# Seven block products instead of eight in both feed-forward layers, the weight sums made on GpSimd

## The reference, cut to what matters

```python
D_MODEL = 1024; SEQ = 512; N_META = 16; D_FF = 2816

def swiglu_ffn(h, w_gate, w_up, w_down):
    return (jax.nn.silu(h @ w_gate) * (h @ w_up)) @ w_down

for i in range(DEPTH):                       # DEPTH = 2
    h = rms_norm(h_res, ln_mix[i])
    mix = s5_mixer(h, ...) if i % 2 == 0 else sink_window_attention(h, ...)
    h_res = h_res + mix
    h_res = h_res + swiglu_ffn(rms_norm(h_res, ln_ffn[i]), w_gate[i], w_up[i], w_down[i])
out = rms_norm(h_res, ln_f)[:, N_META:]
```

## Time and profile before

| | |
|---|---|
| median of three runs | 1177.77 us (1177.47 to 1181.88) |
| span of the profiled execution | 1177.9 us |
| PE busy | 1140.4 us, 97% |
| PE weight loads | 1025.8 us, 87% |
| DVE busy | 553.8 us, 47% |
| ACT busy | 412.4 us, 35% |
| POOL busy | 174.8 us, 15% |
| layer 0's feed-forward, first product to last | about 239 to 628 us |
| layer 1's feed-forward | about 807 to 1168 us |
| share of PE's product line in the chain that ended last | 79% |

### The profile page before, as it was taken

One profiled execution on the slowest core, in us unless ns is written; L12 is line 12 of the kernel. 1 busy time (PEld: TensorE's weight loads), 2 busy tenths in 40 slices (PEclk: granted clock), 3 DMA queues, 4 the chain that ended last, 5 costly groups with the idle time before them and its releaser, 6 DMA issues.

```text
span 1177.9 us, 20443 instructions
## 1 busy us (share of the span) xinstructions
PE 1140.4 (97%) x8362; PEld 1025.8 (87%) x8362; DVE 553.8 (47%) x845; ACT 412.4 (35%) x701; POOL 174.8 (15%) x114
## 2 busy tenths in 40 slices
PE   5799999999999999999999899989999999999998
PEld 5688899999999999999999676678888888888887
DVE  7978444443344333444334355455443434434444
ACT  6823232332222222233323455443322223223332
POOL 4699000011111111100000000001111111110000
PEclk9999899999999999999999999999999999999999
DMA  7164333222323232222323211022333233223332
GB/s 141 24 163 111 87 109 108 72 89 91 98 80 100 78 107 71 76 83 91 98 81 126 72 37 42 32 72 72 108 107 99 79 107 107 75 73 97 98 98 94
DMA packets 119387, 104.63 MB, mean 89 GB/s; under 512 B 21868, under 2 KB 117216, under 8 KB 119008
## 3 DMA queue, kind: packets, MB, share of 16 engines
q1 hardware_dynamic: 110120, 99.85, 27.9%
q10 hardware_dynamic: 9216, 4.06, 1.5%
HBM read 98.11 MB, written 5.24 MB: 88 GB/s over the span
## 4 chain that ended last, share of the span: by engine, by line
PE 90%; DVE 4%; DMA 2%; ACT 1%; POOL 1%; issue 1%; SPq 0%; ACTq 0%; DVEq 0%; POOLq 0%
PE banks L1380 79%; PE banks L1520 1%; PE banks L1457 1%; PE banks L1510 1%; PE banks L1731 1%; PE banks L1734 1%; PE banks L1752 1%; PE banks L1721 1%; PE banks L1458 1%; DMA y_dram<-y_act 1%; PE banks L1746 1%; PE banks L1472 0%; POOL col_mag L499 0%; PE banks L1720 0%; ACTq L719 0%
## 5 line engine op out<-in xcount | busy, mean ns | idle before, releaser
L587 ACT CAST w_high<-raw 128x1024 fp32r<-128x1024 f32 x186 | 195.0, 1049 | 572.1 <-PE banks L1380 572.1
L945 DVE TENSOR_TENSOR w_low<-raw,w_high 128x1024 fp32r<-128x1024 f32 x186 | 228.2, 1228 | 208.3 <-ACT w_high L587 208.3
L1380 PE MATMUL banks<-x_high,w_high 128*128 128x512 f32 (+2 forms) x1184 | 321.0, 324 | 1.0 <-DVE x_low L1173 1.0
L1380 PE MATMUL banks<-x_high,w_low 128*128 128x512 f32 (+2 forms) x1184 | 318.5, 322 | 0.0
L1380 PE MATMUL banks<-x_low,w_high 128*128 128x512 f32 (+2 forms) x1184 | 317.7, 321 | 0.0
L1380 PEld LDWEIGHTS banks<-x_high,w_high 128*128 128x128 f32 x1184 | 198.9, 189 | 19.4 <-issue 2.2
L1380 PEld LDWEIGHTS banks<-x_low,w_high 128*128 128x128 f32 x1184 | 198.9, 188 | 16.1
L1380 PEld LDWEIGHTS banks<-x_high,w_low 128*128 128x128 f32 x1184 | 198.2, 188 | 16.8
L1380 PE MATMUL banks<-a_high,w_high 128*128 128x256 f32 (+2 forms) x533 | 141.2, 318 | 0.0
L1380 PE MATMUL banks<-a_low,w_high 128*128 128x256 f32 (+2 forms) x533 | 141.1, 318 | 0.0
L1380 PE MATMUL banks<-a_high,w_low 128*128 128x256 f32 (+2 forms) x533 | 141.1, 318 | 0.0
(11 more groups left out here) (288 smaller groups left out, 1249.3 us busy)
## 6 DMA issues: line engine op xcount, KB each, us to landing
raw<-in_ffn_w_gate SPq DMA_DIRECT2D x22, 1024.0 KB, 5.3
raw<-in_ffn_w_up SPq DMA_DIRECT2D x22, 1024.0 KB, 5.3
raw<-in_ffn_w_down SPq DMA_DIRECT2D x16, 768.0 KB, 4.4
raw<-in_ffn_w_down SPq DMA_DIRECT2D x16, 640.0 KB, 4.1
raw<-in_attn_w_qkv SPq DMA_DIRECT2D x6, 1024.0 KB, 5.0
k_toep<-k_dram SPq DMA_DIRECT2D x64, 64.0 KB, 2.6
raw<-in_ssm_w_glu_b SPq DMA_DIRECT2D x4, 1024.0 KB, 5.5
raw<-in_ssm_w_glu_a SPq DMA_DIRECT2D x4, 1024.0 KB, 5.8
```

The source lines that it names most:

```text
L587: nc.scalar.copy(high[:, j], raw[:, slot, :, j * P:(j + 1) * P]).then_inc(w_rounded, 1)
L945: nc.vector.tensor_tensor(low[:, j], raw[:, slot, :, j * P:(j + 1) * P], high[:, j], ALU.subtract).then_inc(w_split, 1)
L1380: ins = nc.tensor.matmul(banks[:, bank + h, b0:b0 + cn], w[:, j, k, :], xx[:, first_k + k, c0 + base:c0 + base + cn], start=start and k == ...
```

## The change

Each feed-forward layer becomes 34 units. A unit is one tile of 2 kp x 256 weights: kp = 4 pairs of input blocks (3 in four of the down units) by a pair of output blocks. The tokens are cut into two halves (264 each in layer 0, 256 in layer 1). So the product of a unit is a 2 x 2 by 2 x 2 block product, and it is made with seven block products in place of eight (the scheme of Strassen, in Winograd's form). With `w` the four blocks (0 and 1 from the first row of blocks, 2 and 3 from the second):

- weights: four block sums: `s13` = (w0 + w1, w3 + w1), `s2` = w0 + w3 + w1, `s4` = w2 + s2, all on GpSimd, next to the plain blocks w0, w2 (the column) and w3 (the corner). All seven are rounded by ScalarE and split by VectorE;
- activations: three plain blocks and four sums or differences (T1 to T4) for each pair of rows, seven slots in `xs_high`, `xs_low` and, between up and down, `a_high`, `a_low`;
- results: ScalarE copies three products out of their banks, VectorE combines them to the four corners of the output.

A layer is staged: four pairs of up units, a down stage over pairs 0 to 2, four pairs of up units, a down stage over pairs 3 to 6, three pairs of up units, a down stage over pairs 7 to 10. A down stage has four units, each adding to two rows of `residual`. A ring of SLOTS = 5 pairs of activations takes the place of 22 kept blocks.

TensorE's order in a unit is column w0, first sum, s2, column w2, second sum, corner, s4. The weight parts have one slot each, so a part of the next unit is rounded when TensorE has done this unit's product with it. GpSimd no longer scales the gate; VectorE does. ScalarE's, VectorE's, GpSimd's and SyncE's loops are unrolled.

The last quad of the mixer's output and the last blocks of the attention's output now also carry the preparation of unit 0 (`round_s2`, `split_s2` and the others), and the input rows are prepared in pairs (`pair_first`, `pair_second`) with seven slots.

The core of the diff:

```diff
+        def blocks_of(g, kp):
+            return raw[:, g % 2, 0:2 * kp, :].rearrange("p (k i) (o c) -> p k (i o) c", i=2, o=2)
...
+            def sums13(g, kp):
+                pool.wait_ge(unit_loaded[g % 2], 16 * (g // 2 + 1))
+                if g >= 1:
+                    pool.wait_ge(t_split, 5 * (g - 1) + (5 if g % UNITS == 1 else 2))
+                w = blocks_of(g, kp)
+                nc.gpsimd.tensor_tensor(s13[:, 0:kp], w[:, :, 0::3, :], w[:, :, 1, :].unsqueeze(2).to_broadcast([P, kp, 2, P]),
+                                        ALU.add).then_inc(s13_made, 1)
+            def sum2(g, kp):
+                pool.wait_ge(s13_made, g + 1)
+                if g >= 1:
+                    pool.wait_ge(t_split, 5 * (g - 1) + 3)
+                    pool.wait_ge(s4_made, g)
+                nc.gpsimd.tensor_tensor(s24[:, 0, 0:kp], blocks_of(g, kp)[:, :, 0, :], s13[:, 0:kp, 1, :], ALU.add).then_inc(s2_made, 1)
+            def sum4(g, kp):
+                pool.wait_ge(s2_made, g + 1)
+                if g >= 1:
+                    pool.wait_ge(t_split, 5 * g)
+                nc.gpsimd.tensor_tensor(s24[:, 1, 0:kp], blocks_of(g, kp)[:, :, 2, :], s24[:, 0, 0:kp], ALU.add).then_inc(s4_made, 1)
...
+            def round_s2(g, kp):
+                if g % UNITS > 0:
+                    act.wait_ge(part_done, 7 * (g - 1) + 3)
+                act.wait_ge(s2_made, g + 1)
+                nc.scalar.copy(w2_high[:, 0, 0:kp, :], s24[:, 0, 0:kp, :]).then_inc(t_rounded, 1)
...
+                def copy_parts(g):
+                    act.wait_ge(part_done, 7 * g + 1)
+                    act.wait_ge(c11_made, g)
+                    nc.scalar.copy(copied_part(0, n), bank_part(Y_BANK[g % 2], n)).then_inc(part_copied, 1)
+                    act.wait_ge(part_done, 7 * g + 2)
+                    act.wait_ge(c22_made, g)
+                    nc.scalar.copy(copied_part(1, n), bank_part(W_BANK[g % 2], n)).then_inc(part_copied, 1)
+                def copy_sum(g):
+                    act.wait_ge(part_done, 7 * g + 3)
+                    act.wait_ge(c21_made, g)
+                    nc.scalar.copy(copied_part(2, n), bank_part(Y_BANK[g % 2], n)).then_inc(part_copied, 1)
+                def prepare(unit):
+                    g, kp = UNITS * layer + unit, pairs_of(unit)
+                    round_s2(g, kp)
+                    round_column(g, kp)
+                    round_sums(g, kp)
+                    round_corner(g, kp)
+                    round_s4(g, kp)
+                def unit_behind_acts(unit, i):
+                    copy_parts(UNITS * layer + unit)
+                    round_acts(i)
+                    copy_sum(UNITS * layer + unit)
+                    round_act_sums(i)
+                    prepare(unit + 1)
+                def up_behind_gate(unit, i):
+                    copy_parts(UNITS * layer + unit)
+                    silu(i)
+                    copy_sum(UNITS * layer + unit)
+                    prepare(unit + 1)
...
+                def gate_unit(i):
+                    g, kp = UNITS * layer + up_unit(i), pairs_of(up_unit(i) + 1)
+                    first_corner(g, gate_part(n, 0, 0))
+                    last_corner(g, gate_part(n, 1, 1))
...
+                    split_column(g + 1, kp)
+                    low_corner(g, gate_part(n, 1, 0))
+                    split_sums(g + 1, kp)
+                    split_s2(g + 1, kp)
...
+                    dve.wait_ge(part_done, 7 * g + 7)
+                    TT(gate_part(n, 0, 1), bank_part(Y_BANK[g % 2], n), rstd_part(n, 1), ALU.mult).then_inc(set_free, 1)
+                    split_corner(g + 1, kp)
+                    split_s4(g + 1, kp)
...
+                    TT(gate_part(n, 0, 0), gate_part(n, 0, 0), rstd_part(n, 0), ALU.mult)
+                    TT(gate[:, 1, 0:n], gate[:, 1, 0:n], rstd_row[:, t0:L], ALU.mult).then_inc(gate_pre, 1)
+                def up_products(i):
...
+                    corner, low, far = (bank_part(b[g % 2], n) for b in (X_BANK, W_BANK, V_BANK))
+                    TT(corner, corner, gate_part(n, 0, 0), ALU.mult)
+                    TT(low, low, gate_part(n, 1, 0), ALU.mult)
+                    mark(TT(far, far, gate_part(n, 1, 1), ALU.mult))
...
+                    TT(act_t[:, 0, 0:h], corner, cross, ALU.subtract).then_inc(act_ready, 1)
+                    TT(act_t[:, 2, 0:h], cross, far, ALU.subtract)
...
+                    STT(act_t[:, 1, 0:h], act_t[:, 0, 0:h], -1.0, far, ALU.mult, ALU.subtract).then_inc(act_ready, 1)
...
+                    TT(act_t[:, 3, 0:h], low, act_t[:, 1, 0:h], ALU.add).then_inc(act_ready, 1)
...
+            def unit_products(g, parity, x, slots, n, first=0, need_b11=None, need_all=None, mean_at=None, spread_at=None):
+                y, w, v = Y_BANK[parity], W_BANK[parity], X_BANK[parity]
+                if first == 0:
+                    pe.wait_ge(set_free, g - 1)
+                pe.wait_ge(t_split, 5 * g + (4 if first == 1 else 1))
+                part(col, 0, x, slots, B11, y, n, start=True, need=need_b11)
...
+                pe.wait_ge(t_split, 5 * g + (5 if first == 1 else 2))
+                part(sums, 0, x, slots, T3, w, n, start=True, need=need_all)
+                pe.wait_ge(t_split, 5 * g + (5 if first == 1 else 3))
+                pe.wait_ge(part_copied, 3 * g + 1)
+                part(w2, 0, x, slots, T2, y, n)
+                part(col, 1, x, slots, B21, v, n, start=True)
...
+                pe.wait_ge(part_copied, 3 * g + 3)
+                part(sums, 1, x, slots, T1, y, n)
+                pe.wait_ge(t_split, 5 * g + (5 if first == 1 else 4))
+                part(w2, 1, x, slots, T4, w, n)
+                pe.wait_ge(t_split, 5 * g + 5)
+                pe.wait_ge(c22_made, g + 1)
+                part(w2, 2, x, slots, B22, y, n)
```

More of the change, by code:

```diff
@@ L798, in _ @@
             for i in range(N_GLU):
                 gated(QUAD_GLU + i, i, ACT.Sigmoid, L)
-                for j in range(2):
-                    updated(2 * i + j, 2 * i + j, L, "ln_ffn0")
+                if i == N_GLU - 1:
+                    round_s2(0, KP)
+                    round_corner(0, KP)
+                    round_s4(0, KP)
+                    act.wait_ge(w_used, 4 * N_GLU - 1)
+                    round_column(0, KP)
+                pair_first(0, i, L, "ln_ffn0")
+                if i == N_GLU - 1:
+                    act.wait_ge(w_used, 4 * N_GLU)
+                    round_sums(0, KP)
@@ L837, in feed_forward @@
                 if layer == 0:
-                    with act.Fori(0, N_DOWN, 1) as i:
-                        down(i, False)
-                else:
-                    with act.Fori(0, N_DOWN - 1, 1) as i:
-                        down(i, False)
-                    for off in range(6):
-                        round_weights(QUAD_DOWN[layer] + 2 * (N_DOWN - 1), 2 + off)
-                    updated(adds0 + KB - 2, KB - 2, n, gain)
-                    for h in range(2):
-                        r_h = half_tokens(h)
-                        act.wait_ge(added, adds0 + KB - 1 + h + 1)
-                        nc.scalar.activation(gate[:, 0, r_h], residual[:, KB - 1, r_h], ACT.Square).then_inc(squared, 1)
@@ L851, in _ @@
-            feed_forward(0, L, N_GLU, KB, 0, "ln_mix1")
+                    for m in range(KB - 2, KB):
+                        normed(m)
+                        squared_of(KB + m, m, n)
+                else:
+                    for q in range(2):
+                        act.wait_ge(last_ready, q + 1)
+                        nc.scalar.activation(last_sq[:, :, q * h:(q + 1) * h], residual[:, KB - 2:, half_tokens(q)],
+                                             ACT.Square).then_inc(squared, 1)
@@ L1618, in last_mean @@
                     nc.tensor.matmul(banks[:, MEAN_BANKS[h], t:t + 1], sq_sum[:, tokens], ones[:, 0:1], start=True, stop=False)
-                    ins = nc.tensor.matmul(banks[:, MEAN_BANKS[h], t:t + 1], gate[:, 0, tokens], ones[:, 0:1], start=False, stop=True)
+                    for j in range(2):
+                        ins = nc.tensor.matmul(banks[:, MEAN_BANKS[h], t:t + 1], last_sq[:, j, t * P:(t + 1) * P], ones[:, 0:1],
+                                               start=False, stop=j == 1)
                 ins.then_inc(mean_summed, 1)
@@ L1688, in _, with part @@
-            feed_forward(0, L, N_GLU, KB, 0, [(gate_ready, 2 * N_GLU - 1), (gate_ready, 2 * N_GLU)])
-            first_quad(QUAD_KV, 1, L, [(added, 2 * KB - 1), (added, 2 * KB)], None)
+            col = (col_high(w_high, KP), col_high(w_low, KP))
+            sums = (sum_high(w_high, KP), sum_high(w_low, KP))
+            w2 = tuple(w[:].rearrange("p s k c -> p k s c") for w in (w2_high, w2_low))
+            def part(w, i, x, slots, c, bank, n, start=False, need=None):
+                for m, slot in enumerate(slots):
+                    if need is not None:
+                        need(m)
+                    for a, b in ((0, 0), (0, 1), (1, 0)):
```

(4 more changed lines are left out.)

716 lines of the change are left out of this document (508 added, 208 removed).

## The result

The changed kernel takes 1377.1 us (median of 4 runs, 1371.9 to 1379.0) against 1179.4 us (4 runs, 1177.5 to 1181.9) for the kernel before on the same chip. The ratio is 1.168, 95% interval 1.165 to 1.171. It is slower, as forecast, but by 198 us where 135 had been forecast, and the time lies 11 us above the range. The profiled execution has a span of 1377.2 us, so it can be read without a shift.

The account below looks back on a forecast made before the run. TensorE was taken to bound the kernel before, and a VectorE-ScalarE-TensorE loop with waits for GpSimd's port the changed one. 1177.9 + 110 (layers) + 10 (outside) + 15 (clock) = 1313 us, range 1215 to 1366.

Parts of the forecast that it names:

- The bound before and TensorE's floor: Feed-forward layers: TensorE bounds the kernel before; its floor after the change is 20.5 us a pair of gate and up units.
- fourth rival: TensorE: narrow products dearer than 0.1219 us through new rows' place in SBUF; result as forecast; chance 0.05.
- first rival: VectorE and GpSimd: the exclusion does not act on this pattern, TensorE is the bound, about 1135 us; chance 0.08.
- The exclusion: VectorE instructions with two SBUF operands wait out whole GpSimd instructions that read SBUF; 7.0 us a pair in the loop.
- second rival: VectorE keeps the port between its own instructions, GpSimd takes what is left; 1222 us; chance 0.15.
- The loop of a pair: VectorE, ScalarE and TensorE's fifth product, per gate and up pair: 20.0 us alone, 27.0 with waits for GpSimd.
- The clock: TensorE drops to half clock after some gaps in up and gate units: 15 us taken, between 0 and 66.
- third rival: TensorE: the clock falls in nearly every gap, 66 us, giving 1364 us; chance 0.12.
- Outside the layers: First unit's preparation +3 us and +4 in layer 1, keys +1, the end +2: 10 us.
- The edges of the stages: Down units: 10.8 us each, 8.9 with three pairs of rows, waits behind GpSimd included.
- What would show it right: Changed profile: TensorE at 75 to 80%, idle before the fifth product; 512-element splits 1.7 to 2.6 us; matmul spacing 0.12.
- The stall before the last down stage: Last down stage of each layer: waits for the newest activations, about 11 us once a layer.

Follow-up runs that it names:

- e1: Changed kernel with every GpSimd weight sum cut to 4 of 128 columns; 1146.4 us, 0.971 of the kernel before.
- e4: Changed kernel with each GpSimd weight sum replaced by three memsets of its tile; 1153.5 us, 0.978 of the kernel before.
- e8: Changed kernel with each GpSimd weight sum replaced by two copies with one SBUF input each; 1234.9 us, 1.049 of the kernel before.
- e2: Changed kernel with 20 filling matmuls ahead of the fifth product of gate and up units but the first two; 1337.7 us, 1.134 of the kernel before.
- e10: Changed kernel with silu over one of the two gate rows, the other left out; 1358.1 us, 1.151 of the kernel before.
- e12: Changed kernel with 12 filling matmuls ahead of the fifth product of gate and up units but the first two; 1335.7 us, 1.132 of the kernel before.

## Why the prediction was right or wrong

- *The bound before and TensorE's floor:* right. With the exclusion gone (e1) the pair takes 20.6 us where 20.5 was worked out, so the narrow products are as cheap as priced and the fourth rival is out. The first rival's 1135 us became 1146 in e1.
- *The exclusion:* right in all its parts. Only a read of GpSimd stops a double read of VectorE (e4, e8), the whole instruction is waited out, and whoever waits goes next: the splits at 2.54 and 1.77 us in the pair shown (2.35 and 1.69 in the mean) against 1.9 and 1.06 on top of 0.60. The second rival (VectorE keeps the port) is refuted by the alternation at 438 to 446 us. By the Trainium skill ("SBUF — State Buffer", section "Who interferes with whom") a GpSimd instruction that only writes SBUF doesn't contend; e4 agrees, with splits at 0.68 us beside 400 us of memsets.
- *The loop of a pair:* right but for silu. I priced it at 0.63 us, the row of 528 elements, though it runs over both gate rows; it takes 1.08 [L1022]. 27.0 + 0.45 = 27.45, and e2, with the clock held, shows 27.4. What this cost in all, with the clock that rose as well, is 19 us in e10.
- *The clock:* the step that failed most, a term of the sum that was mis-sized. "I take 15, as these gaps follow full-length work": 32 of 40 were followed by half clock all the same, 229 us in all, and removing most of it gave 39 to 41 us (e2, e12). That is 24 of the 64 us between 1313 and 1377. The reason I gave for the low value came from no row; the one row I had of such a gap was against it. (The trace of before has two longer waits, 6.16 us up to 26.70 and 4.27 us up to 33.08. Its record of the clock starts only at 44.0 us, so they decide nothing.) The third rival named this, at 66 us. Its chance should have been the larger. That its 1364 us lies only 13 below the measured time is luck: it priced the clock too high and lacks silu's length and the edges. More than the fifth product lies in the slow stretch (24 matmuls from 416.65 take 5.66 us in the chain, 0.236 each), so VectorE's third corner waits for the sixth too; that slow matmuls elsewhere stood beside a late VectorE and cost nothing is argued, not shown.
- *The range:* its upper end, 1366, took the clock's whole swing (51 us) but not the 12 us for dearer sums beside it. Both together would have ended at 1376.
- *Outside the layers:* 10 us forecast, 13 measured (1377.2 - 466 - 466 against 1177.9 - 386 - 360), and 6 in e2 (1333.7 - 453 - 443).
- *The edges of the stages:* under-priced. A down unit was given 10.8 us, or 8.9 with three pairs of rows. Behind the last pair of a stage the first down unit still carries half of the pair's loop. Starts of ScalarE's first copy in the changed kernel, second down stage of layer 0:

```profile
514.26 0.38 ACT L999 COPY parts<-banks 128x264 f32<-128x264 f32 x1 [0.84 <-PE banks L2156]
...
528.77 0.38 ACT L999 COPY parts<-banks 128x264 f32<-128x264 f32 x1 [0.85 <-PE banks L2156]
...
539.11 0.38 ACT L999 COPY parts<-banks 128x264 f32<-128x264 f32 x1 [0.85 <-PE banks L2156]
...
550.14 0.38 ACT L999 COPY parts<-banks 128x264 f32<-128x264 f32 x1 [0.85 <-PE banks L2156]
...
561.16 0.38 ACT L999 COPY parts<-banks 128x264 f32<-128x264 f32 x1 [0.83 <-PE banks L2156]
```

  The four take 14.5, 10.3, 11.0 and 11.0 us. By the same starts in e2, with the clock held, the first down units of the first two stages (12.2, 14.8, 11.3 and 14.7 us) and the last but one down unit of each layer (14.8 and 13.0; VectorE makes the norm's squares and the next input in it) exceed the forecast by 13.6 + 6.2 = 20 us.

In sum: 1313 - 15 for the clock is 1298. e2, with most of the clock's loss gone, is 1338: 10 for silu's length, 20 for the edges, and 10 that I have not placed. The 20 are the largest items, not a full account: in e2 the first pair of each layer also takes 3 to 5 us more than a steady one, and the stalls before the two last down stages take 14.3 us where 22 were forecast. The clock adds 39: 1377. The half clock that e2 leaves (80 us, where e1 has 50 and before 14) wasn't removed, so the clock's full share stays open; 39 us is what could be shown. "What would show it right" held for the splits, the sums, the spacing and TensorE's idle place. The stall before the last down stage was up to 7.0 us where 11 was forecast, and TensorE's share in the layers is 82% with the slow matmuls counted as busy.

## What to carry to other kernels

When work is given to GpSimd, list the VectorE instructions that read two operands from SBUF and lie in its reach: each pays up to one whole GpSimd instruction, and if VectorE is in a loop with TensorE the kernel pays it too. Before moving the work elsewhere, move it in time, next to VectorE's instructions with an operand in PSUM; here one wait's constant was worth 143 us, and operands kept in PSUM the last 15. Price a recurring TensorE gap with the half clock that such a gap in the trace is followed by, over all products that lie in the slow stretch, and don't set the price near nothing for a reason that no row shows.

## What the runs showed of the hardware

- GpSimd writing SBUF costs VectorE nothing (0.68 us splits beside memsets of 0.96 and 0.53 us); reading one operand stops it as reading two does (splits at 1.14 and 1.44 us beside copies of 0.7 to 1.4 us).
- When both have work queued, GpSimd and VectorE take turns instruction by instruction, and the wait lies inside the recorded duration: 2.54 us for a split that takes 0.68 alone.
- Half clock follows most recurring gaps of 2 to 4 us, not all (32 of 40). It cost less at the end than its matmuls say: of 229 us at half clock, taking 149 away gave some 40 us, and 12 filling matmuls gave as much as 20.
- In this loop, which ends in a TensorE gap, a saving counted about twice: 9.7 us of silu gave 19 (one run).
